# Transposing the first rows as they land, sparse attention's output by token tiles behind two kept product tiles, and three changed orders

## The reference, cut to what matters

```python
h = rmsnorm(x, norm_mix_g)
proj = h @ w_in              # c_q, c_kv, k_r, q_b, k_b, v_b, q_i, k_i, w_i, g_a, g_b
o_a = chunk_causal_attention(q_a, k_a, v_a, 96 ** -0.5)        # 8 heads, 4 blocks of 128 queries
score = sum_h(w_i[h] * relu(q_i[h] @ k_i.T / 8)), -inf outside the causal chunks
_, sel = top_k(score, 128)
o_b = softmax(q_b @ k_b[sel].T / 8) @ v_b[sel]
y = sigmoid(g_a) * (o_a @ w_o_a) + sigmoid(g_b) * (o_b @ w_o_b)
x = x + y @ w_out
```

## Time and profile before

| what | us |
|---|---|
| three timed runs, median (lowest, highest) | 1928.31 (1925.71, 1930.79) |
| the profiled execution, own time | 1927.32 |
| its span, first to last instruction | 1925.7 |
| PE busy | 1870.6 (97%) |
| DVE busy | 1179.9 (61%) |
| ACT busy | 1040.1 (54%) |
| share of PE in the chain that ended last (DVE, DMA) | 71% (16%, 6%) |
| PE's granted clock in the entry, 0 to 20 us | 1.00 |

### The profile page before, as it was taken

One profiled execution on the slowest core, in us unless ns is written; L12 is line 12 of the kernel. 1 busy time (PEld: TensorE's weight loads), 2 busy tenths in 40 slices (PEclk: granted clock), 3 DMA queues, 4 the chain that ended last, 5 costly groups with the idle time before them and its releaser, 6 DMA issues.

```text
span 1925.7 us, 27345 instructions
## 1 busy us (share of the span) xinstructions
PE 1870.6 (97%) x10047; PEld 1626.2 (84%) x10047; DVE 1179.9 (61%) x2466; ACT 1040.1 (54%) x1810; POOL 377.7 (20%) x453
## 2 busy tenths in 40 slices
PE   7999999999999999899999999999999999999998
PEld 7977877778787877689999999999888787778887
DVE  3335389754799999875444554455343645957972
ACT  5654543444588887765555554555443555445440
POOL 2601233101100100132113322133020102412310
PEclk9999999999999999999999999999999999999999
DMA  4411222118699999932323233323343522122131
GB/s 155 143 54 45 66 66 74 48 56 285 213 367 354 370 369 355 326 110 58 91 84 93 83 84 91 92 83 109 90 136 127 164 66 77 56 66 77 55 110 44
DMA packets 187312, 259.44 MB, mean 135 GB/s; under 512 B 14605, under 2 KB 101594, under 8 KB 187178
## 3 DMA queue, kind: packets, MB, share of 16 engines
q1 hardware_dynamic: 178048, 225.56, 36.6%
q0 software_dynamic: 8720, 31.59, 4.3%
q10 hardware_dynamic: 410, 0.52, 0.1%
HBM read 239.24 MB, written 14.16 MB: 132 GB/s over the span
## 4 chain that ended last, share of the span: by engine, by line
PE 71%; DVE 16%; DMA 6%; ACT 4%; issue 2%; POOL 1%; SPq 1%; ACTq 0%; DVEq 0%; POOLq 0%
PE pb L2609 51%; DVE wlo L1713 6%; PE pb L2636 5%; DMA wraw<-w_down 2%; PE pb L2987 2%; PE pb L2695 2%; ACT whi L1056 2%; PE pb L2708 2%; PE pb L3121 1%; PE pb L3229 1%; DMA wraw<-w_up 1%; DVE arena L1965 1%; PE pb L2876 1%; DVE small L1964 1%; PE pb L3012 1%
## 5 line engine op out<-in xcount | busy, mean ns | idle before, releaser
L2609 PE MATMUL pb<-whi,AT_hi 128*128 128x512 f32 (+4 forms) x1864 | 722.4, 388 | 4.3 <-ACT arena L1500 1.4
L1713 DVE TENSOR_TENSOR wlo<-wraw,whi 128x1024 fp32r<-128x1024 f32 (+4 forms) x430 | 494.6, 1164 | 309.8 <-ACT whi L1056 306.9
L2609 PE MATMUL pb<-whi,AT_lo 128*128 128x512 f32 (+4 forms) x1864 | 675.3, 362 | 0.0
L2609 PE MATMUL pb<-wlo,AT_hi 128*128 128x512 f32 (+4 forms) x1864 | 673.7, 361 | 0.0
L1056 ACT ACTIVATE whi<-wraw 128x1024 fp32r<-128x1024 f32 (+4 forms) x446 | 440.6, 995 | 362.6 <-PE pb L2609 304.9
L2609 PEld LDWEIGHTS pb<-whi,AT_hi 128*128 128x128 f32 x1864 | 351.2, 188 | 46.0 <-issue 11.4
L2609 PEld LDWEIGHTS pb<-wlo,AT_hi 128*128 128x128 f32 x1864 | 351.6, 189 | 39.1 <-issue 6.5
L2609 PEld LDWEIGHTS pb<-whi,AT_lo 128*128 128x128 f32 x1864 | 350.2, 188 | 39.5
L2636 PE MATMUL pb<-arena 128*128 128x128 f32 (+1 forms) x1044 | 158.1, 276 | 16.6 <-DMA arena<-x_all,arena 5.6
L2636 PEld LDWEIGHTS pb<-arena 128*128 128x128 f32 (+1 forms) x1044 | 129.7, 145 | 48.0 <-issue 8.7
L1036 POOL TENSOR_TENSOR arena<-arena 128x256 f32<-128x256 f32 x72 | 71.5, 999 | 179.7 <-ACT arena L1646 166.4
(11 more groups left out here) (353 smaller groups left out, 2601.5 us busy)
## 6 DMA issues: line engine op xcount, KB each, us to landing
wraw<-w_in_a SPq DMA_DIRECT2D x288, 128.0 KB
wraw<-w_gate SPq DMA_DIRECT2D x128, 256.0 KB
wraw<-w_up SPq DMA_DIRECT2D x128, 256.0 KB
wraw<-w_down SPq DMA_DIRECT2D x58, 512.0 KB
wraw<-w_in_b SPq DMA_DIRECT2D x40, 512.0 KB
wraw<-w_in SPq DMA_DIRECT2D x28, 512.0 KB
wraw<-w_mem_kv SPq DMA_DIRECT2D x16, 512.0 KB
wraw<-w_in_a SPq DMA_DIRECT2D x16, 512.0 KB
```

What stands on the lines that cost most here:

```text
L1713: dve.tensor_tensor(w_slot(wlo, p, p % SPL), raw_slot(p), w_slot(whi, p, p % SPL).bitcast(F32), ALU.subtract).then_inc(lo_done[p % SPL], 1)
L2609: mm = pe.matmul(ACC[bank][:, 0:n], a, b, start=kc == 0 and q == 0, stop=i == c["count"] - 1 and kk == per - 1 and q == 2)
```

## The change

Entry: PE multiplies a zero tile eleven times at first; the norm's gain is fetched and transposed alone; each block of rows is transposed when it lands, units 0 to 5 into the banks ACC[0..3], TP[0], TP[1]; the other gains follow. Attention: ACT copies an output out of PSUM before it feeds a weight piece; DVE's second feed of qkvb0 moves behind MLA's unit 0. oa: one top-k round moves from before the products to behind the first. The mask's last step becomes a scalar_tensor_tensor. Sparse attention: units 4 and 11 have no product tile; tiles 32 and 33 come behind the last units, and o_b is transposed and split by token tiles between them and ob0.

```diff
@@ -442,6 @@
 mg_d, mg_e, mg_l = (stat(2 * NT).rearrange("p (g t) -> p g t", g=2) for _ in range(3))
...
+WARM = 11
+warm = work[:, 2176:2304]
+def first_t(k):
+    return ACC[k] if k < 4 else TP[k % 2]
@@ -708,6 @@
...
 BESIDE_DSA = tiles_of("gb0", "gb1")
+for i in (4, 11):
+    BESIDE_DSA.insert(i, None)
@@ -1166,10 @@
...
+            if i:
+                out_of_psum(i - 1)
             if i >= 2:
                 feed_beside(tiles[i - 2])
-            if i:
-                out_of_psum(i - 1)
         feed_beside(tiles[n - 1])
@@ -1247,7 @@
...
     act.dma_start(ident, A["const"][:, 0:P]).then_inc(S("ident_in"), 16)
-    for at, src in ((0, A["norm_mix_g"]), (8, A["mla_q_norm_g"]), (11, A["mla_kv_norm_g"]), (13, A["norm_ffn_g"]),
+    act.dma_start(gain_rows[0:8, :], A["norm_mix_g"].rearrange("l (k p) -> (l k) p", p=P)).then_inc(S("ident_in"), 16)
+    for at, src in ((8, A["mla_q_norm_g"]), (11, A["mla_kv_norm_g"]), (13, A["norm_ffn_g"]),
@@ -1260,14 @@
...
     act.wait_ge(S("gains_t"), 1)
-    act.activation(gains[:, 0:61], SC[0][:, 0:61], ACT.Copy).then_inc(S("gains_ready"), 1)
+    act.activation(gains[:, 0:8], SC[0][:, 0:8], ACT.Copy).then_inc(S("gains_ready"), 1)
     act.wait_ge(S("gains_ready"), 1)
     for k in range(KD):
-        hi("n1", k, AT_hi[:, k, :], tb("n1", k), g_mix[:, k:k + 1])
-        if k in (1, 2, 4, 5):
-            feed((1, 2, 4, 5).index(k))
-        if k in (2, 4):
-            x_square(k // 2 + 1)
+        hi("n1", k, AT_hi[:, k, :], first_t(k), g_mix[:, k:k + 1])
+        if k in (0, 2, 4, 6):
+            feed(k // 2)
+        if k == 3:
+            act.wait_ge(S("gains_t"), 2)
+            act.activation(gains[:, 8:61], SC[1][:, 8:61], ACT.Copy).then_inc(S("gains_ready"), 1)
+        if k in (3, 5):
+            x_square((k + 1) // 2)
...
     for i in range(2):
@@ -1358,12 @@
     for i in range(2):
...
-    attention_beside("dsa", dsa_unit, 32, BESIDE_DSA, (("gb0", gb[0], (14, 15, 16, 17)),))
+    attention_beside("dsa", dsa_unit, 32, BESIDE_DSA, (("gb0", gb[0], (16, 17, 18, 19)),))
     wait_used(act, "oa1")
-    for k in range(4):
-        hi("ob", k, AT_hi[:, 8 + k, :], tb("ob", k))
-        wait_acc(act, CH["gb1"], k)
-        act.activation(gb[1][:, k, :], ACC[k], ACT.Copy, scale=n1_rs[:, k:k + 1]).then_inc(acc_free[k], 1)
+    for t in range(NT):
+        hi("ob", t, AT_hi[:, 8:12, P * t:P * t + P], tb("ob", t).rearrange("p (k c) -> p k c", k=4))
+        wait_acc(act, CH["gb1"], t)
+        act.activation(gb[1][:, t, :], ACC[t], ACT.Copy, scale=n1_rs[:, t:t + 1]).then_inc(acc_free[t], 1)
+    feed_beside(BESIDE_DSA[33])
     for i in range(2):
         for t in range(NT):
@@ -1916,12 @@
...
+    link(dve.memset(warm, 0.0))
     dve.wait_ge(S("gains_ready"), 1)
+    for k in range(KD):
+        lo("n1", k, AT_lo[:, k, :], first_t(k), AT_hi[:, k, :], g_mix[:, k:k + 1])
+        if k in (0, 2, 4, 6):
+            feed(k // 2)
+    dve.wait_ge(S("gains_ready"), 2)
     dve.tensor_tensor(g_n2[0], g_n2[0], g_fin, ALU.mult).then_inc(S("g_both"), 1)
-    for k in range(KD):
-        lo("n1", k, AT_lo[:, k, :], tb("n1", k), AT_hi[:, k, :], g_mix[:, k:k + 1])
-        if k in (1, 2, 4, 5):
-            feed((1, 2, 4, 5).index(k))
@@ -1946,9 @@
...
     flow("uk")
-    for q in range(2):
-        feed(chunks[CH["qkvb0"]]["first"] + q + SPL)
-    attention_beside("mla", mla_unit, 32, BESIDE_MLA, lambda i: None)
+    feed(chunks[CH["qkvb0"]]["first"] + SPL)
+    attention_beside("mla", mla_unit, 32, BESIDE_MLA,
+                     lambda i: None if i else feed(chunks[CH["qkvb0"]]["first"] + 1 + SPL))
     for k in range(4):
@@ -1965,7 @@
...
             if r == ROUNDS - 1:
                 link(dve.tensor_tensor(sc, left, sc, ALU.is_equal))
-                link(dve.tensor_scalar(sc, sc, NEG, None, ALU.mult))
+                link(dve.scalar_tensor_tensor(sc, sc, NEG, sc, ALU.mult, ALU.min))
@@ -1999,15 @@
...
                     dve.tensor_tensor(y, ACC[t][:, :], y, ALU.mult).then_inc(acc_free[t], 1)
+                    if t == 0:
+                        kept_back = min(1, early - done)
+                        top_rounds(done, kept_back)
+                        done += kept_back
             feed(chunks[j]["first"] + q + SPL)
-            more = min(some, early - done)
+            more = min(some - (name[0] == "o" and q == 0), early - done)
             top_rounds(done, more)
             done += more
     top_rounds(done, early - done)
     attention_beside("dsa", dsa_unit, 32, BESIDE_DSA,
                      lambda i: top_rounds(early + i - 2, 1) if 2 <= i < 2 + ROUNDS else None)
-    for k in range(4):
-        lo("ob", k, AT_lo[:, 8 + k, :], tb("ob", k), AT_hi[:, 8 + k, :])
+    for t in range(NT):
+        cols = slice(P * t, P * t + P)
+        lo("ob", t, AT_lo[:, 8:12, cols], tb("ob", t).rearrange("p (k c) -> p k c", k=4), AT_hi[:, 8:12, cols])
+    feed_beside(BESIDE_DSA[33])
@@ -2794,22 @@
...
+    def rows_in(t):
+        pe.wait_ge(S(f"x_in{t}"), 16)
+        for k in range(6):
+            tr = pe.transpose(first_t(k)[:, P * t:P * t + P], xr[:, t, P * k:P * k + P], ident)
+            if t == NT - 1:
+                tr.then_inc(tp_ready, 1)
...
-    pe.wait_ge(S("ident_in"), 16)
-    pe.wait_ge(S("gains_in"), 112)
-    pe.transpose(SC[0][:, 0:61], gain_rows[0:61, :], ident[0:61, 0:61]).then_inc(S("gains_t"), 1)
+    pe.wait_ge(S("dve_step"), 1)
+    for _ in range(WARM):
+        pe.matmul(SC[1][:, 0:P], warm, warm, start=True, stop=True)
+    pe.wait_ge(S("ident_in"), 32)
+    pe.transpose(SC[0][:, 0:8], gain_rows[0:8, :], ident[0:8, 0:8]).then_inc(S("gains_t"), 1)
     for t in range(NT):
-        pe.wait_ge(S(f"x_in{t}"), 16)
-    for k in range(4):
-        n1_t(k)
+        rows_in(t)
+    pe.wait_ge(S("gains_in"), 96)
+    pe.transpose(SC[1][:, 0:61], gain_rows[0:61, :], ident[0:61, 0:61]).then_inc(S("gains_t"), 1)
     for i in range(4):
         ready("n1", (2 * i, 2 * i + 1))
         for t in range(NT):
+            if i == 0:
+                ready("n1", (t,))
             project_tile("cqkv0", i, t)
-            if i < 2 and t % 2:
-                n1_t(4 + 2 * i + t // 2)
+            if i == 1 and t % 2:
+                n1_t(6 + t // 2)
@@ -2882,11 @@
...
+    def ob_t(t):
+        transposes("ob", t, [o_tokb[:, t, P * k:P * k + P] for k in range(4)])
     attention_beside("dsa", dsa_unit, 32, BESIDE_DSA)
-    wait_tp_read(pe, "dsa", 32)
-    for k in range(4):
-        transposes("ob", k, [o_tokb[:, t, P * k:P * k + P] for t in range(NT)])
-    project("ob0", "ob")
+    ob_t(0)
+    project_tile(*BESIDE_DSA[33])
+    ob_t(1)
+    for t in range(3):
+        ready("ob", (t,))
+        project_tile("ob0", 0, t)
+        if t < 2:
+            ob_t(t + 2)
+    project_tile("ob0", 1, 0)
+    ready("ob", (3,))
+    project_tile("ob0", 0, 3)
+    for t in range(1, NT):
+        project_tile("ob0", 1, t)
...
```

## The result

The changed kernel took 1935.49 us (median of 9 runs, 1932.30 to 1939.37), the kernel before 1928.35 beside it (9 runs). The ratio is 1.0033, 95% interval 1.0023 to 1.0044: slower by 0.33%. I had forecast 1924.7, with a range of 1920.5 to 1929.5. The profiled execution took 1938.19 itself, with a span of 1936.5.

A forecast was written before the change was run, and what follows sets the result against it. PE (TensorE), busy 97% of the span, was taken as the bound, with DVE a second bound in sparse attention. Terms -2.3 - 1.5 - 0.15 - 1.8 + 2.2 = -3.6 gave 1924.7 us, range 1920.5 to 1929.5.

The forecast's parts named there:

- The premise past 430 us: Expert stage: nothing is edited there, weights are issued as ring slots come free, so the rest shifts as a whole.
- Entry: Start to first project pieces: earlier first tile, fewer transposes between pieces, array fast by 12.9; -2.3 us, bounds -2.8 and +0.6.
- That rival: Entry: 2.7 us of PE idle before the first tile brings the slow pace; 1930, chance 0.08 shared with another loss.
- MLA's start: Start of MLA attention: DVE's weight split behind unit 0 removes PE's wait; -1.5 us, bounds -1.7 and -0.9.
- ScalarE's order: MLA attention: ACT's output copy ahead of its weight split leaves no further wait to take; 0 (+-0.2) us.
- oa0/oa1: Before sparse attention: PE arrives early but waits for DVE, whose mask step still meets POOL; -0.15 us, bounds -0.9 and +0.5.
- Units 2 to 17: Sparse attention: DVE sets the pace; shifted feeds keep POOL's subtraction off the mask step; -1.8 us, bounds -2.9 and 0.
- Tail: Last probability transpose to ob1: ACT's sigmoids finish late and PE waits 1.9 us; +2.2 us, bounds +0.3 and +2.8.
- Absorbed by the weight stream: Rival: the expert stage, with DMA at 95%, ends when it did; 1928.3, chance 0.13.

The follow-up runs named there:

- pad44: Kernel before with 88 idle waits (44 instructions) added at TensorE's start; 1935.33 us against 1929.04, ratio 1.0035.
- no_warm: Changed kernel without its eleven warm products; 1929.63 us against 1929.16 for the kernel before, ratio 1.0002.
- entry_only: Kernel before with the entry's edits alone, warm products included; 1933.98 us against 1929.32, ratio 1.0021.
- fill_gap: final with the eleven warm products back and 20 more zero products ahead of the first tile; 1924.03 us against 1928.32 for the kernel before.
- fill_both: final with the eleven warm products back, 5 zero products behind the first rows and 16 ahead of the first tile; 1924.11 us, ratio 0.9978.
- picked: Changed kernel with the old entry, ScalarE's old order, and gb0's products ahead of VectorE's weight split in the tail; 1927.66 us against 1929.04.
- final: picked with the new entry but no warm products; 1924.47 us against 1929.16 for the kernel before, ratio 0.9978.

## Why the prediction was wrong

The forecast was 3.6 us of gain, the result 7.1 us of loss. Two groups of steps failed.

**The premise past 430 us.** The sum took for granted that "Past 430 nothing is edited" and "the rest shifts as a whole". That holds for the work and not for the program text. The eleven warm products put 44 instructions ahead of the experts' branch, and the branch then took 6.2 us in place of 0.38, with a block fetch inside it. pad44 shows that 44 instructions alone cost 6.3 us (4.2 to 9.3 by its interval); no_warm that without them the change is at +0.5, which is not clear of zero (-1.5 to +2.5). Of pad44's 6.3, its ledger has 5.4 across the branch: the idle time (5.1 us against 1.7) and the last eight products, at the lower clock (5.77 us against 3.71; 6.38 in entry_only). In all five kernels with a fetch inside the branch, a fall of the clock for 6.8 us begins inside that idle time; in none of the others do these products run at the lower clock. Another 0.4 to 3.1 us come behind 830, in part as waits on v_near, a DMA. They do not belong to the long branch: fill_gap and fill_both, with 124 and 128 added instructions and a branch under 0.5 us, lose 1.4 and 1.8 us there and wait on the same DMA (0.6 and 1.0). In entry_only one instruction block's fetch, at 1303.4, took 1.51 us, and v_near's last part landed 1.5 behind the others; that the one delayed the other is argued from this, not shown. The rest is within the spread of executions.

**The edited stages.** At 430 us the changed kernel stood at +0.96 where -3.6 was forecast, so 4.6 of the miss lie in the sum's own terms: the entry's pace and ScalarE's order in MLA. Even without the branch the forecast gain would not have come, as no_warm shows.

By the prediction's own steps:

- **Entry, -2.3.** The order worked: first tile 12.9 forecast, 13.02 measured. The pace did not: I let the array be fast by 12.9 because of the warm products, and priced 2.7 us of idle time only as a rival. The clock fell in all five new entries without work in the gap (to 0.5 for 3.4 to 6.8 us), and their ledgers read -0.8 to +0.5. That rival was right about the place; of its 35 to 50 slow products some 21 came in the changed kernel, and their 0.28 in place of 0.155 cost 2.6. Against it the prediction said that the trace shows no second fall. It shows one, in the 0.99 of the earlier trace rows: from 506.6 us the granted clock is at its lower level for 6.8 us, after TensorE had stood idle for 2.0 us, made eighteen narrow products, and begun to wait for 1.1 more. With ten zero products in the gap the entry gives -2.44.
- **MLA's start, -1.5.** Measured -1.55 (0.50 to -1.05). Right.
- **ScalarE's order, 0 +- 0.2.** Wrong: +1.8 in MLA. "Pieces are fed three ahead" looked at the weights; what counted was VectorE's half of the split, standing in front of a maximum. In sparse attention, where it was to shorten nothing, it gained 0.7 on VectorE's chain, in small steps. The order for that stage alone was not tried.
- **oa0/oa1, -0.15.** Right in kind: TensorE came 0.75 us early and waited 0.9 for L1164, +0.05 in all. As forecast, the comparison met GpSimd's subtraction, longer than forecast (2.37, to 307.0, not 305.6); the mask behind it took 0.56:

```profile
304.14 2.40 POOL L920 TENSOR_TENSOR wlo<-wraw,whi 128x1024 fp32r<-128x1024 f32 x1 [3.27 <-ACT whi L1063]
...
304.59 2.37 DVE L1981 TENSOR_TENSOR arena<-arena 128x384 f32<-128x384 f32 x1
307.00 0.56 DVE L1982 SCALAR_TENSOR_TENSOR arena<-arena 128x384 f32<-128x384 f32 x1
```

- **Units 2 to 17, -1.8.** Measured -1.9 (+0.8 to -1.1), in part by luck. The reason given, the mask (0.69 at 353.95, away from GpSimd), brought about 1.25, as in picked and final; the other 0.7 came from ScalarE's order.
- **Tail, +2.2.** Measured +2.1, wait 1.9. Right, and avoidable by one moved feed.
- **Absorbed by the weight stream.** No rule of this kind shows: in picked's trace the 2.1 us brought to the expert stage were gone by 760, while final kept its 3.4.
- **The range, 1920.5 to 1929.5.** It was said to come from the terms' bounds. Their upper ends sum to +3.2 us, which is 1931.5; the measured 1935.5 lies outside that too.

MLA's start, oa0/oa1, units 2 to 17 and the tail came within 0.2 us, one of them by luck. Those that failed assumed something that no row showed.

## What to carry to other kernels

An added instruction has a cost beside its time: it shifts the code behind it. Where a program has a branch, read the branch's record, and the block fetches beside it, before and after any edit that changes the count, and try such an edit against the same count of idle instructions. Keep the array at work up to the first tile, not only early: fill the last gap, and count the passes that a product really makes. And before a clock of 1.00 is read from a view, compare the distance between starts with it.

## What was new about the hardware

- A taken branch 275 instructions forward (by the count in the program) took 0.36 to 0.45 us or 5.95 to 6.23, by where it stood. The Trainium skill, Runtime: NRT & Kernel Launch, section "Instruction fetch mechanics", says: "A taken branch whose target isn't in the current 2-page window forces a DMA fetch of the target page before execution can continue". The traces agree: one 16 KB fetch inside each branch of 6 us, none in one of under 0.5. It took 1.1 us, but it started 3.4 to 3.8 us into the branch and was over 1.4 us before the branch's end, so most of the stall lies ahead of the transfer. Where the exact border lies (between 22 and 44 added, and again between 76 and 124) stays open.
- In all five new entries without work in the gap the granted clock fell to its lower level, 1.2 GHz, after TensorE's last transposes (from 12.4 to 14.6 us on, idle 2.47 in the changed kernel); with zero products in the gap it stayed at 1.00 in all three.
- At the start TensorE ran at its slow pace until the trace's clock record begins: at 15.1 us in the kernel before, 7.4 in entry_only, 10.7 in no_warm, 5.5 in the changed kernel. The distance between starts falls to about half where the record begins (0.21 to 0.11 for a transpose, 0.28 to 0.155 for 336 columns). The views read 1.00 ahead of it.
